# Latent attention with its queries prepared two heads ahead, and three kinds of small jobs handed to GpSimd

## The chip, the cores and the metric

The kernel runs on one core of a Trainium2 chip. The metric is device microseconds (us) of one execution, the median over several executions. One more execution was recorded by the hardware profiler; its trace gives the start and the length of nearly every instruction on each engine.

Five engines work side by side, each in the order of its own program: PE (TensorE) multiplies matrices and transposes, DVE (VectorE) and ACT (ScalarE) do the arithmetic on vectors, POOL (GpSimd) can do such arithmetic on data in SBUF too, and SP (SyncE) issues the transfers. They meet at semaphores: an instruction waits until a named counter has reached a value, and counts another one up when it is done.

## The reference: what is computed

The program is a four-layer transformer (256 latent tokens, 256 context tokens, width 1024), followed by a second block with 16 experts. The third layer's mixer is latent attention, and only that is touched:

```python
def mla_project(h, w_down, q_norm_g, kv_norm_g, w_uq, w_ukv, rope):
    cq, ckv, k_rope = jnp.split(h @ w_down, [MLA_Q_RANK, MLA_Q_RANK + MLA_KV_RANK], axis=-1)
    q = (rms_norm(cq, q_norm_g) @ w_uq).reshape(b, s, MLA_HEADS, MLA_NOPE_DIM + MLA_ROPE_DIM)
    kv = (rms_norm(ckv, kv_norm_g) @ w_ukv).reshape(b, s, MLA_HEADS, MLA_NOPE_DIM + MLA_V_DIM)
    ...
def mla_attend(q_nope, q_rope, k_nope, k_rope, v):
    scale = (MLA_NOPE_DIM + MLA_ROPE_DIM) ** -0.5
    s = (jnp.einsum("bqhd,bkhd->bhqk", q_nope, k_nope)
         + jnp.einsum("bqhr,bkr->bhqk", q_rope, k_rope)).astype(jnp.float32) * scale
    p = jax.nn.softmax(s, axis=-1)
    return jnp.einsum("bhqk,bkhe->bqhe", p.astype(v.dtype), v)
```

There are 16 heads. Each has 256 queries (two tiles of 128 rows) and 512 keys. The head outputs are then multiplied by `mla_w_o`.

## The kernel before: one turn per head, on four engines

**Exact products in three passes.** Each operand x is split into a high part (a rounded copy of type fp32r, made by ACT) and a low part (x minus the high part, made by DVE). A product is hi x hi + lo x hi + hi x lo: the three matmul lines L1847, L1848 and L1849. So every operand that is made on the way costs one ACT instruction and one DVE instruction. The weights are treated in the same way, in panels of 128x1024: `split_hi` (ACT, L1064) writes `w_hi`, `split_lo` (DVE, L2818) writes `w_lo` and counts up `panel_ready`. For that counter PE waits before it uses a panel, and SP before it loads new weights into the raw buffer.

**The turns.** `mla_attention` exists on ACT (L1532 on), PE (L2347 on) and DVE (L3451 on), and its order is written out by hand. Turn h belongs to head h:

- DVE takes the row maxima of both score tiles (`m_max`, L3493).
- ACT takes the exponentials (`mp_raw`, L1569), with the row sums beside them.
- DVE inverts the sums (`m_zinv`, L3502, counts up `z_inv`) and scales row tile 0 in place (L3504, `mla_norm0`). ACT scales row tile 1 in place (L1577, `mla_norm1`). PE waits for both before it transposes the weights (L2396).
- In the same turn the query of head h+1 is prepared: PE multiplies it out, DVE applies the rotary table (`mq_f`, L3461), ACT copies it (`mq_hi`, L1542), DVE subtracts (`mq_lo`, L3465). There is one buffer of each. Then PE can start the scores of head h+1.
- In turns 0 to 13 half of a pair of key tiles follows (`mk_hi` L1547, `mk_lo` L3471), then the output of head h-2 (`g_hi` L1583, `g_lo` L3514), then the two halves of the transposed weights of head h-1 (`mpt_hi` L1592, `mpt_lo` L3522).
- At the end of some turns stand value tiles (`h_hi` L1551, `h_lo` L3477; two in turns 0 and 1, one in turns 3 to 6) and weight panels (`splits`: turns 0, 1, 3, 6, 8, 14 and 15, one each).

PE's order in a turn: scores of head h, query of head h+1, keys (in even turns), weighted values of head h-2, transposes of head h-1, values. Scores and transposes each alternate between two PSUM banks, so that the scores of head h+1 may not be written before the exponentials of head h are taken. Query and value products share two banks. After turn 15 PE goes on with the weighted values of head 14 and, head pair by head pair, with the product with `mla_w_o` (`out_products`).

POOL has 8 subtractions in the first layer; in this layer 16 small copies and two subtractions before turn 0. After that it is idle to the end of the layer. DVE and POOL touch the same buffers nowhere in the turns.

## Time and profile before

| | us |
|---|---|
| median of 3 executions (2012.34 to 2015.85) | 2015.19 |
| the profiled execution, its own time | 2013.53 |
| its span, from the first to the last instruction | 2011.8 |
| PE busy | 1921.9 (96%) |
| DVE busy | 1531.0 (76%) |
| ACT busy | 1018.4 (51%) |
| POOL busy | 22.5 (1%) |
| from the first row maximum of turn 0 to that of turn 15, read at 1152.14 and 1250.07 | 97.93 |
| in these 97.93: DVE, PE and ACT busy | 82.57, 81.63, 71.96 |

All times in the text are microseconds from the start of the span. Busy times are sums over an engine's instructions; ends of matmuls are modelled, and consecutive instructions of one engine overlap a little in the record, so that the distance from start to start says more than the length. Over the whole program PE is busy for 96%; in the turns of this layer it is not, and the next section but one shows whom each engine waits for.

### The profile page before, as it was taken

How to read it: one execution, taken by the hardware profiler on the slowest of the kernel's cores; microseconds unless marked ns; L12 is line 12 of the kernel's file. 1: busy time of each engine (PE TensorE's matmuls, PEld its weight loads, DVE VectorE, ACT ScalarE, POOL GpSimd, SP SyncE). 2: the span in 40 equal slices, each digit the busy share in tenths (PEclk: the TensorE clock that was granted, in tenths of full speed). 3: DMA queues.
4: the chain of work that ended last, by engine and by line, in shares of the span. 5: the costliest groups of instructions: out<-in, count | busy, mean ns of one | idle time of the engine just before them, and what ended most of it. 6: DMA issues, size and time to landing. Idle time of an engine off the chain costs nothing.

```text
span 2011.8 us, 31051 instructions
## 1 busy us (share of the span) xinstructions
PE 1921.9 (96%) x11602; PEld 1684.5 (84%) x11602; DVE 1531.0 (76%) x2619; ACT 1018.4 (51%) x1721; POOL 22.5 (1%) x40
## 2 busy tenths in 40 slices
PE   6889999999999999999999777999999999999998
PEld 4687888889787888888888667999999999997886
DVE  3689888887667758777777588788887667876796
ACT  5353323245666656232333577655555546655685
POOL 0200000000000000000000100000000000000000
PEclk9999999999999999999999899999999999999999
DMA  7936455541211234557675220677645555426795
GB/s 291 321 119 232 165 209 188 188 168 48 84 64 63 67 112 139 169 186 244 236 244 158 58 73 27 227 268 261 207 135 189 168 169 168 134 67 236 260 354 195
DMA packets 265319, 346.67 MB, mean 172 GB/s; under 512 B 24167, under 2 KB 234962, under 8 KB 263778
## 3 DMA queue, kind: packets, MB, share of 16 engines
q1 hardware_dynamic: 265186, 344.90, 51.2%
q8 instruction: 84, 1.38, 0.3%
q14 instruction: 49, 0.40, 0.1%
HBM read 343.81 MB, written 1.06 MB: 171 GB/s over the span
## 4 chain that ended last, share of the span: by engine, by line
PE 75%; DVE 10%; ACT 6%; issue 5%; SPq 1%; DMA 1%; DVEq 0%; ACTq 0%
PE bank L1847 23%; PE bank L1848 23%; PE bank L1849 23%; PE bank L2663 2%; DVE w_lo L2818 2%; PE bank L2653 1%; ACT p_raw L1401 1%; ACT p_raw L1389 1%; DVE p_all L3297 1%; ACT norm L1157 1%; ACT w_hi L1064 1%; ACT mp_raw L1569 1%; DVE x L2886 1%; DVE neg_max L3306 1%; DVE norm L2844 1%
## 5 line engine op out<-in xcount | busy, mean ns | idle before, releaser
L2818 DVE TENSOR_TENSOR w_lo<-w_raw,w_hi 128x1024 fp32r<-128x1024 f32 x449 | 545.6, 1221 | 51.6 <-ACT w_hi L1064 24.9
L1064 ACT ACTIVATE w_hi<-w_raw 128x1024 fp32r<-128x1024 f32 x350 | 368.0, 1053 | 381.7 <-PE bank L1849 371.2
L1847 PE MATMUL bank<-h_hi,w_hi 128*128 128x512 f32 (+3 forms) x1360 | 466.9, 343 | 14.7 <-DVE w_lo L2818 8.6
L1848 PE MATMUL bank<-h_lo,w_hi 128*128 128x512 f32 (+3 forms) x1360 | 460.3, 338 | 0.0
L1849 PE MATMUL bank<-h_hi,w_lo 128*128 128x512 f32 (+3 forms) x1360 | 459.9, 338 | 0.0
L1847 PE MATMUL bank<-g_hi,w_hi 128*128 128x256 f32 (+1 forms) x1216 | 401.6, 330 | 7.2 <-DVE g_lo L3351 3.6
L1848 PE MATMUL bank<-g_lo,w_hi 128*128 128x256 f32 (+1 forms) x1216 | 399.6, 329 | 0.0
L1849 PE MATMUL bank<-g_hi,w_lo 128*128 128x256 f32 (+1 forms) x1216 | 399.5, 329 | 0.0
L1847 PEld LDWEIGHTS bank<-h_hi,w_hi 128*128 128x128 f32 x1360 | 257.9, 190 | 50.5 <-DVE w_lo L2818 10.8
L1849 PEld LDWEIGHTS bank<-h_hi,w_lo 128*128 128x128 f32 x1360 | 258.1, 190 | 27.7
L1848 PEld LDWEIGHTS bank<-h_lo,w_hi 128*128 128x128 f32 x1360 | 258.2, 190 | 26.4 <-issue 0.3
L1847 PEld LDWEIGHTS bank<-g_hi,w_hi 128*128 128x128 f32 x1216 | 231.8, 191 | 30.2 <-DVE g_lo L3351 4.5
L1849 PEld LDWEIGHTS bank<-g_hi,w_lo 128*128 128x128 f32 x1216 | 231.8, 191 | 20.3
L1848 PEld LDWEIGHTS bank<-g_lo,w_hi 128*128 128x128 f32 x1216 | 231.9, 191 | 19.7
L2971 DVE CUSTOM_DVE_ANT_0 mod_raw<-mod_raw,c_all,vec 128x1024 f32<-128x1024 f32 x160 | 203.0, 1278 | 0.0
L3016 DVE SCALAR_TENSOR_TENSOR x<-bank,mod,x 128x256 f32<-128x256 f32 x192 | 87.4, 479 | 85.1 <-PE bank L1849 79.8
L1304 ACT ACTIVATE norm<-bank 128x512 f32<-128x512 f32 x64 | 38.3, 598 | 189.4 <-PE bank L1849 189.4
L1744 ACT ACTIVATE w_hi<-w_raw 128x1024 fp32r<-128x1024 f32 x99 | 104.1, 1059 | 33.8 <-PE bank L1849 22.5
L3164 DVE TENSOR_TENSOR norm<-norm 128x512 f32<-128x512 f32 (+1 forms) x128 | 71.0, 555 | 54.2 <-ACT norm L1304 49.6
L2971 DVE CUSTOM_DVE_ANT_0 mod_prod<-mod_raw,c_all,vec 128x1024 f32<-128x1024 f32 x80 | 102.2, 1277 | 0.0
L3167 DVE TENSOR_TENSOR g_lo<-norm,g_hi 128x512 fp32r<-128x512 f32 (+1 forms) x128 | 71.5, 559 | 13.6 <-DVE norm L3164 0.5
L1847 PE MATMUL bank<-u_hi,w_hi 128*128 128x258 f32 x256 | 73.5, 287 | 0.0
(535 smaller groups left out, 2832.0 us busy)
## 6 DMA issues: line engine op xcount, KB each, us to landing
w_raw<-in_mlp_w SPq DMA_DIRECT2D x128, 1024.0 KB, 5.4
mod_raw<-in_mod_t SPq DMA_DIRECT2D x80, 1024.0 KB, 7.3
w_raw<-in_w_expert_gate SPq DMA_DIRECT2D x34, 512.0 KB, 4.7
w_raw<-in_w_expert_up SPq DMA_DIRECT2D x34, 512.0 KB, 5.8
w_raw<-in_w_expert_down SPq DMA_DIRECT2D x17, 1024.0 KB, 5.7
first_raw<-in_mod_w SPq DMA_DIRECT2D x16, 1024.0 KB, 5.9
w_raw<-in_diff_w_qkv SPq DMA_DIRECT2D x12, 1024.0 KB, 5.2
w_raw<-in_fourier_w SPq DMA_DIRECT2D x8, 1024.0 KB, 7.9
```

What stands on the lines that cost most here:

```text
L1064: act.activation(split_panel(W_hi[n % RING], n), raw_panel(n), ACT.Copy).then_inc(s("w_hi"), 1)
L1304: act.activation(relu[j % 2][:, 0:n_cols], bank[(t0 + j) % BANKS][:, 0:n_cols], ACT.Relu).then_inc(s("relu"), 1)
L1744: act.activation(W_hi[(p0 + n) % RING][:, :], raw_panel(p0 + n), ACT.Copy).then_inc(s("w_hi"), 1)
L1847: pe.matmul(dst, w_hi, r_hi, start=start, stop=False)
L1848: pe.matmul(dst, w_hi, r_lo, start=False, stop=False)
L1849: return pe.matmul(dst, w_lo, r_hi, start=False, stop=stop)
L2663: ins = pe.matmul(slot_out[half][:, :], e[x % 2][:, k, 0:P], v[:, w], start=x % 4 == 0 and k == 0 and q == 0, stop=x % 4 == 3 and k == 1 a ...
L2818: dve.tensor_tensor(split_panel(W_lo[n % RING], n), raw_panel(n), split_panel(W_hi[n % RING], n).bitcast(F32), ALU.subtract).then_inc(s("p ...
L2971: dve.tensor_tensor_reduce(mod_prod[:, :] if again else raw, raw, c_all[:, st, :], 1.0, bias, ALU.mult, ALU.add, mod[layer][:, t, st:st + ...
L3016: ins = dve.scalar_tensor_tensor(X[:, m, c], bank[t % BANKS][:, c], mod[layer][:, gate_at + m, st:st + 1], X[:, m, c], ALU.mult, ALU.add)
L3164: dve.tensor_tensor(squared, relu[j % 2][:, c], relu[j % 2][:, c], ALU.mult).then_inc(s("g_sq"), 1)
L3167: dve.tensor_tensor(G_lo[:, j, c], squared, G_hi[:, j, c].bitcast(F32), ALU.subtract).then_inc(s("g_lo"), 1)
```

## The change

Three things are done.

1. Queries two heads ahead. `mq_f`, `mq_hi` and `mq_lo` become two buffers each. Query 1 is made before turn 0, and turn h makes query h+2, on PE, DVE and ACT alike. On DVE the rotary product of head h waits for the subtraction of head h-2.
2. The second normalization (row tile 1, `mla_norm1`) moves from ACT to POOL: 16 instructions.
3. The low parts of the seven weight panels of this stage move from DVE to POOL, each behind the normalization of its turn. DVE waits for the last of them before the residual update behind the attention.

```diff
@@ mla_tiles
     add("q", 0, "mla_q", 1)
     add("k", 0, "mla_k_lo", 2)
-    for turn in range(MLA_HEADS - 1):
-        add("q", turn + 1, "mla_q", turn + 2)
+    add("q", 1, "mla_q", 2)
+    for turn in range(MLA_HEADS - 2):
+        add("q", turn + 2, "mla_q", turn + 3)
...
+MLA_SPLITS = {0: [2], 1: [3], 3: [4], 6: [5], 8: [6], 14: [7], 15: [8]}
...
@@ GpSimd
             swap_rotary(u + 2, 1)
+            p0 = PLAN.at["mla"]["panel"]
+            pool.wait_ge(s("panel_ready"), p0 + 2)
+            for turn in range(MLA_HEADS):
+                pool.wait_ge(s("z_inv"), BEFORE_MLA["z_inv"] + turn + 1)
+                pool.tensor_scalar(mp_raw[turn % 2][1][:, :], mp_raw[turn % 2][1][:, :], m_zinv[:, turn % 2, 1:2], None,
+                                   ALU.mult).then_inc(s("mla_norm1"), 1)
+                for n in MLA_SPLITS.get(turn, []):
+                    r = (p0 + n) % RING
+                    pool.wait_ge(s("w_hi"), p0 + n + 1)
+                    pool.tensor_tensor(split_panel(W_lo[r], p0 + n), raw_panel(p0 + n), split_panel(W_hi[r], p0 + n).bitcast(F32),
+                                       ALU.subtract).then_inc(s("panel_ready"), 1)
@@ ScalarE
                 query(0)
+                query(1)
                 for turn in range(MLA_HEADS + 2):
...
-                    if turn + 1 < MLA_HEADS:
-                        query(turn + 1)
+                    if turn + 2 < MLA_HEADS:
+                        query(turn + 2)
                     if turn // 2 + 1 < MLA_HEADS // 2:
                         keys(turn // 2 + 1, turn % 2)
-                    if on:
-                        act.wait_ge(s("z_inv"), BEFORE_MLA["z_inv"] + turn + 1)
-                        act.activation(mp_raw[turn % 2][1][:, :], mp_raw[turn % 2][1][:, :], ACT.Identity,
-                                       scale=m_zinv[:, turn % 2, 1:2]).then_inc(s("mla_norm1"), 1)
@@ TensorE
                 query_spread()
+                query(1)
                 for turn in range(MLA_HEADS):
                     scores(turn)
-                    if turn + 1 < MLA_HEADS:
-                        query(turn + 1)
+                    if turn + 2 < MLA_HEADS:
+                        query(turn + 2)
@@ VectorE
                 def query(h):
                     dve.wait_ge(s("tile_done"), t0 + MLA_TILE_AT["q", h] + 1)
-                    if h:
-                        dve.wait_ge(s("qk_lo"), BEFORE_MLA["qk_lo"] + h)
+                    if h >= 2:
+                        dve.wait_ge(s("qk_lo"), BEFORE_MLA["qk_lo"] + h - 1)
...
                 for j in range(2):
                     keys(0, j)
+                query(1)
+                query_lo(1)
...
-                    if turn + 1 < MLA_HEADS:
-                        query(turn + 1)
+                    if turn + 2 < MLA_HEADS:
+                        query(turn + 2)
...
-                    if turn + 1 < MLA_HEADS:
-                        query_lo(turn + 1)
+                    if turn + 2 < MLA_HEADS:
+                        query_lo(turn + 2)
...
-                    for n in splits.get(turn, []):
-                        split_lo_at(p0 + n)
...
             dve.memset(norm_buf[3][:, LAT:LAT + 2], 1.0).then_inc(s("down_inv"), 1)
+            dve.wait_ge(s("panel_ready"), PLAN.at["mla"]["panel"] + 9)
             output_added("mlao", 2, 1)
```

DVE in the first two turns, before. Each row is one instruction (x2: two in a row): line, operation, what is written from what. Numbers behind a name tell buffers apart:

```order
L3465 TENSOR_TENSOR mq_lo<-mq_f,mq_hi 128x256
L3471 TENSOR_TENSOR mk_lo_154<-bank,mk_hi_152 64x512
L3471 TENSOR_TENSOR mk_lo_155<-bank,mk_hi_153 64x512
L3493 TENSOR_REDUCE m_max<-bank 128x1 x2
L3461 TENSOR_TENSOR mq_f<-bank,q_table 128x256
L3502 RECIPROCAL m_zinv<-m_z 128x2
L3504 TENSOR_SCALAR mp_raw_140<-mp_raw_140,m_zinv 128x512
L3465 TENSOR_TENSOR mq_lo<-mq_f,mq_hi 128x256
L3471 TENSOR_TENSOR mk_lo_154<-bank,mk_hi_152 64x512
L3477 TENSOR_TENSOR h_lo<-bank,h_hi 128x512 x2
L2818 TENSOR_TENSOR w_lo_63<-w_raw_68,w_hi_59 128x1024
L3493 TENSOR_REDUCE m_max<-bank 128x1 x2
```

The same place on DVE in the changed kernel (its line numbers are a little higher):

```order
L3485 TENSOR_TENSOR mk_lo_158<-bank,mk_hi_156 64x512
L3474 TENSOR_TENSOR mq_f_150<-bank,q_table 128x256
L3478 TENSOR_TENSOR mq_lo_154<-mq_f_150,mq_hi_152 128x256
L3508 TENSOR_REDUCE m_max<-bank 128x1 x2
L3474 TENSOR_TENSOR mq_f_149<-bank,q_table 128x256
L3517 RECIPROCAL m_zinv<-m_z 128x2
L3519 TENSOR_SCALAR mp_raw_140<-mp_raw_140,m_zinv 128x512
L3478 TENSOR_TENSOR mq_lo_153<-mq_f_149,mq_hi_151 128x256
L3485 TENSOR_TENSOR mk_lo_157<-bank,mk_hi_155 64x512
L3491 TENSOR_TENSOR h_lo<-bank,h_hi 128x512 x2
L3508 TENSOR_REDUCE m_max<-bank 128x1 x2
```

A second query stands ahead of the first maxima, `mq_lo` keeps its place directly behind the scaling of row tile 0, and the panel subtraction is gone from the end of the turn.

POOL in the changed kernel, from its last small copies to the end of turn 3. Before, nothing stands between these copies and the next layers' work:

```order
L1027 COPY w_raw_66<-w_raw_66 128x4x2x8 x8
L1048 TENSOR_SCALAR mp_raw_141<-mp_raw_141,m_zinv 128x512
L1053 TENSOR_TENSOR w_lo_63<-w_raw_68,w_hi_59 128x1024
L1048 TENSOR_SCALAR mp_raw_143<-mp_raw_143,m_zinv 128x512
L1053 TENSOR_TENSOR w_lo_64<-w_raw_65,w_hi_60 128x1024
L1048 TENSOR_SCALAR mp_raw_141<-mp_raw_141,m_zinv 128x512
L1048 TENSOR_SCALAR mp_raw_143<-mp_raw_143,m_zinv 128x512
L1053 TENSOR_TENSOR w_lo_61<-w_raw_66,w_hi_57 128x1024
```

So POOL scales once per turn, when `z_inv` is counted up, which is what DVE's own scaling of row tile 0 waits for as well; a panel subtraction delays the scaling of the next turn if it takes too long.

## Rows read from the trace of the kernel before

**Rows 1.** Waits, 1140 to 1285: engine and line waited for whom; us, times, longest
```profile
ACT mp_raw L1569 <- DVE m_max L3493: 27.6, 17, 2.3
PEld bank L1847 <- DVE mq_lo L3465: 21.1, 15, 3.2
DVE m_zinv L3502 <- ACT mp_raw L1569: 9.4, 16, 0.9
DVE m_max L3493 <- PE bank L1849: 1.7, 2, 1.1
```

**Rows 2.** DVE's timeline, turns 10 to 12: start, us, instruction, [idle before it <- releaser]
```profile
1220.30 1.28 DVE L3493 TENSOR_REDUCE m_max<-bank 128x1 f32<-128x512 f32 x2
...
1225.85 1.28 DVE L3493 TENSOR_REDUCE m_max<-bank 128x1 f32<-128x512 f32 x2
...
1228.05 0.17 DVE L3502 RECIPROCAL m_zinv<-m_z 128x2 f32<-128x2 f32 x1 [0.59 <-ACT mp_raw L1569]
1228.25 0.49 DVE L3504 TENSOR_SCALAR mp_raw<-mp_raw,m_zinv 128x512 f32<-128x512 f32 x1
1228.65 0.42 DVE L3465 TENSOR_TENSOR mq_lo<-mq_f,mq_hi 128x256 fp32r<-128x256 f32 x1
1229.10 0.69 DVE L3471 TENSOR_TENSOR mk_lo<-bank,mk_hi 64x512 fp32r<-64x512 f32 x1
1230.12 0.43 DVE L3514 TENSOR_TENSOR g_lo<-bank,g_hi 64x256 fp32r<-64x256 f32 x1 [0.33 <-ACT g_hi L1583]
1230.74 1.29 DVE L3522 TENSOR_TENSOR mpt_lo<-bank,mpt_hi 128x512 fp32r<-128x512 f32 x2 [0.19 <-ACT mpt_hi L1592]
1231.95 1.28 DVE L3493 TENSOR_REDUCE m_max<-bank 128x1 f32<-128x512 f32 x2
```

**Rows 3.** ACT's timeline in turn 11
```profile
1228.96 0.72 ACT L1577 ACTIVATE mp_raw<-mp_raw,m_zinv 128x512 f32<-128x512 f32 x1
```

**Rows 4.** DVE's timeline, the panel subtraction that ends turn 8
```profile
1213.05 1.22 DVE L2818 TENSOR_TENSOR w_lo<-w_raw,w_hi 128x1024 fp32r<-128x1024 f32 x1
1214.20 1.28 DVE L3493 TENSOR_REDUCE m_max<-bank 128x1 f32<-128x512 f32 x2
```

**Rows 5.** DVE's timeline, the first maxima of turn 0 and those of turn 15
```profile
1152.14 0.69 DVE L3493 TENSOR_REDUCE m_max<-bank 128x1 f32<-128x512 f32 x1 [1.07 <-PE bank L1849]
...
1250.07 1.28 DVE L3493 TENSOR_REDUCE m_max<-bank 128x1 f32<-128x512 f32 x2
```

**Rows 6.** POOL's timeline, where DVE works on SBUF at the same time
```profile
58.81 2.79 POOL L1027 TENSOR_TENSOR h_lo<-norm,h_hi 128x512 fp32r<-128x512 f32 x2 [3.09 <-ACT h_hi L1254]
...
1137.60 1.30 POOL L1035 TENSOR_TENSOR mk_lo<-kr_f,mk_hi 64x512 fp32r<-64x512 f32 x1
```

**Rows 7.** DVE's timeline at the same times
```profile
59.97 1.92 DVE L3051 SCALAR_TENSOR_TENSOR g_lo<-four_raw,scale_mix,g_hi 128x254 fp32r<-128x254 f32 x2 [1.10 <-ACT g_hi L1237]
...
1137.96 1.50 DVE L3432 TENSOR_TENSOR ckv_lo<-ckv_f,ckv_hi 128x512 fp32r<-128x512 f32 x1 [0.70 <-ACT ckv_hi L1518]
```

**Rows 8.** Single lines: count, shortest/median/longest ns, first and last start
```profile
L3051 DVE SCALAR_TENSOR_TENSOR g_lo<-four_raw,scale_mix,g_hi x16: 468/480/1518, 43.2 to 62.2; 128x254 fp32r<-128x254 f32 x16
L1022 POOL COPY w_raw<-w_raw x16: 231/233/1235, 1107.0 to 1142.6; 128x64 f32<-128x64 f32 x16
```

**Rows 9.** POOL's groups by line: busy us, mean ns | idle before
```profile
L1043 POOL TENSOR_SCALAR_AFFINE_SELECT qs<-qs 64x512 f32<-64x512 f32 x2 | 1.3, 657 | 597.0 <-ACT qs L1692 597.0
L1005 POOL MEMSET silu_c<- 128x256 f32 x1 | 0.3, 313 | 0.0
L1002 POOL MEMSET ones<- 128x128 f32 x1 | 0.2, 206 | 0.0
```

**Rows 10.** Timelines of ACT and PE behind the maxima of turn 15
```profile
1254.59 1.06 ACT L1064 ACTIVATE w_hi<-w_raw 128x1024 fp32r<-128x1024 f32 x1
...
1255.08 0.36 PE L1847 MATMUL bank<-mpt_hi,h_hi 128*128 128x256 f32 x1 [4.21 <-DVE mpt_lo L3522]
...
1258.40 0.41 PE L1847 MATMUL bank<-g_hi,w_hi 128*128 128x256 f32 x1
```

More of the change, by code:

```diff
@@ L559, in build_program @@
         ckv_hi, ckv_lo = sb("ckv_hi", [P, TOK], F32R), sb("ckv_lo", [P, TOK], F32R)
-        mq_f = sb("mq_f", [P, LAT])
-        mq_hi, mq_lo = sb("mq_hi", [P, LAT], F32R), sb("mq_lo", [P, LAT], F32R)
+        mq_f = [sb(f"mq_f{j}", [P, LAT]) for j in range(2)]
+        mq_hi = [sb(f"mq_hi{j}", [P, LAT], F32R) for j in range(2)]
+        mq_lo = [sb(f"mq_lo{j}", [P, LAT], F32R) for j in range(2)]
         mk_hi = [sb(f"mk_hi{j}", [P, TOK], F32R) for j in range(2)]
@@ L1541, in query @@
                     act.wait_ge(s("mla_q"), h + 1)
-                    act.activation(mq_hi[:, :], mq_f[:, :], ACT.Copy).then_inc(s("qk_hi"), 1)
+                    act.activation(mq_hi[h % 2][:, :], mq_f[h % 2][:, :], ACT.Copy).then_inc(s("qk_hi"), 1)
                 def keys(pair, j):
@@ L1595, in mla_attention @@
                         values(i)
-                    for n in splits.get(turn, []):
+                    for n in MLA_SPLITS.get(turn, []):
                         if n == 4:
@@ L2385, in scores @@
                         q = slice(i * P, (i + 1) * P)
-                        split_product(dst[:, :], mq_hi[:, q], mq_lo[:, q], mk_hi[h % 2][:, :], mk_lo[h % 2][:, :],
+                        split_product(dst[:, :], mq_hi[h % 2][:, q], mq_lo[h % 2][:, q], mk_hi[h % 2][:, :], mk_lo[h % 2][:, :],
                                       True, True).then_inc(s("aux_done"), 1)
@@ L3458, in query @@
                     dve.wait_ge(s("tile_done"), t0 + MLA_TILE_AT["q", h] + 1)
-                    if h:
-                        dve.wait_ge(s("qk_lo"), BEFORE_MLA["qk_lo"] + h)
-                    dve.tensor_tensor(mq_f[:, :], made("q", h)[:, 0:LAT], q_table[:, h % 2, :], ALU.mult).then_inc(s("mla_q"), 1)
+                    if h >= 2:
+                        dve.wait_ge(s("qk_lo"), BEFORE_MLA["qk_lo"] + h - 1)
+                    dve.tensor_tensor(mq_f[h % 2][:, :], made("q", h)[:, 0:LAT], q_table[:, h % 2, :], ALU.mult).then_inc(s("mla_q"), 1)
                 def query_lo(h):
                     dve.wait_ge(s("qk_hi"), BEFORE_MLA["qk_hi"] + h + 1)
-                    dve.tensor_tensor(mq_lo[:, :], mq_f[:, :], mq_hi[:, :].bitcast(F32), ALU.subtract).then_inc(s("qk_lo"), 1)
+                    dve.tensor_tensor(mq_lo[h % 2][:, :], mq_f[h % 2][:, :], mq_hi[h % 2][:, :].bitcast(F32),
+                                      ALU.subtract).then_inc(s("qk_lo"), 1)
                 def keys(pair, j):
@@ L3478, in values @@
                                       ALU.subtract).then_inc(s("v_lo"), 1)
-                splits = {0: [2], 1: [3], 3: [4], 6: [5], 8: [6], 14: [7], 15: [8]}
                 query(0)
@@ L3524, in mla_attention @@
                         values(i)
-                    for n in splits.get(turn, []):
-                        split_lo_at(p0 + n)
             norm_rest("mix2", TOK)
```

1 line of the change is left out of this document (removed).

## The prediction, made before the changed kernel ran

> **What bounds the kernel now.** Read the busy shares first: PE 96% over the program, so that most edits off PE are worth nothing. Then read them for the stage that is changed. From the first maxima of turn 0 to those of turn 15 [rows 5] lie 97.93 us, of which PE is busy for 81.63 and DVE for 82.57: nobody is full there, so a loop over several engines sets the pace. The waits of this stretch show which [rows 1]. PE waits for `mq_lo` for 21.1 us, which looks like the bound, but DVE waits for PE's scores only twice, 1.7 us in all: PE is early whatever the query costs. ACT waits 27.6 us for `m_max`, and DVE 9.4 us in 16 waits for the exponentials. So the loop is DVE to ACT and back to DVE, with everything else that DVE must do in a turn.
>
> DVE's timeline shows the turn [rows 2]. Turn 10 takes 1225.85 - 1220.30 = 5.55, turn 11 takes 1231.95 - 1225.85 = 6.10. Counted from the maxima: inversion of the sums at 2.20, after 0.59 of idling for the exponentials; scaling of row tile 0 at 2.40; `mq_lo` at 2.80; `mk_lo` at 3.25; `g_lo` at 4.27 after 0.33 of waiting for ACT; `mpt_lo` after 0.19 more. In turn 10 these last two waits are missing. They exist because ACT has its own normalization, 0.72 us long, ahead of `g_hi` and `mpt_hi` [rows 3].
>
> **The change, part by part.**
>
> *Normalization off ACT.* ACT reaches `g_hi` about 0.6 to 0.7 earlier. The waits of 0.33 and 0.19 go, and a turn like 11 becomes one like 10: 0.55 each. What is late next is DVE itself.
>
> *Panel subtractions off DVE.* From its start to the next maxima one takes 1214.20 - 1213.05 = 1.15 [rows 4]. Six of the seven end turns ahead of turn 15 (0, 1, 3, 6, 8, 14), 6.9 us, with some tenths of waiting for `w_hi` in front; ACT's part stays, and lies in its idle time before the next exponentials.
>
> *Queries two ahead.* PE may begin scores earlier, but DVE hardly waits for them, so by itself this is worth nothing on DVE's path. It has a use as cover: with ACT faster, transposes would be late next, as they follow the scores on PE; now the scores need not wait for `mq_lo`. Ahead of turn 0 DVE gets one query more, some 0.7 us, in the 1.07 that it idles there [rows 5]; nothing. Turn 14 loses its query.
>
> I rebuild the 15 turns instead of adding differences: 15 x 5.55 = 83.25. Eight value tiles at 0.60 (half of the 1231.95 - 1230.74 = 1.21 for the two equal subtractions of rows 2) add 4.8. Turn 0 has no `g_lo` and no `mpt_lo`, but waits for PE's second scores: -1.1. Turn 1 has no `g_lo`: -0.5. Turn 14 has neither query nor keys: -1.1. Sum 85.35, against 97.93: a gain of 12.6, if POOL's work were free.
>
> *What POOL costs DVE.* It is not free, and this is the term that I rest most on. POOL subtracted from 1137.60 to 1138.90 [rows 6]; DVE's `ckv_lo`, both inputs in SBUF, began at 1137.96 and took 1.50 [rows 7], where two equal subtractions with one input in PSUM take 1.29 together. It ended 0.56 behind POOL's end, so it stood still to 0.13 before that end. In the first layer POOL's pair of subtractions ran from 58.81 to 61.60, and two of DVE's L3051 from 59.97 to 61.89; the second of them took 1.518 instead of the median 0.480 [rows 6 to 8], so that it began at 60.37. And POOL's copies, 0.231 each, took up to 1.235 [rows 8]. So one of the two stands still while the other works on SBUF. The second case shows more: POOL's first subtraction was over at about 60.1, DVE's first instruction ran, and then POOL's second subtraction got in ahead of DVE's second instruction. The Trainium skill ("SBUF — State Buffer", "Who interferes with whom") states this as a rule: a VectorE instruction with two SBUF inputs, or one in a two-port mode, and a GpSimd instruction that reads SBUF exclude each other for the whole instruction. By that rule, with which the trace agrees, work moved to GpSimd is not free where VectorE is the bound.
>
> In each turn POOL's normalization is released by the same `z_inv` as DVE's scaling, and behind that stands `mq_lo`, with both inputs in SBUF. The scaling does 512 columns in 0.49, where a subtraction of 512 takes 0.65 to 0.69, so it runs in a faster mode and I take it to exclude POOL too. Then: scaling 2.40 to 2.89; POOL's normalization gets in; `mq_lo` stands still. Should POOL come first, the scaling stands still instead, with the same sum. How long? The trace of before has no such operation on POOL. Nearest rows [rows 9]: 512 elements with one input, the selection on 64 rows, 0.657; memsets of 128 and 256 elements 0.206 and 0.313, so 0.84 ns an element and 0.10 fixed, 0.53 for 512. As its start-up lies beside the scaling, I let it end 0.5 behind the scaling, at 3.39, and `mq_lo` start again 0.15 before that: 3.24 instead of 2.80, x = 0.45. The lower end is x = 0 (no exclusion, or `mq_lo` slips in first); the upper end the two-input subtraction's 1.30 in full: 2.89 + 1.30 - 0.15 - 2.80 = 1.24. I take 0.45, since it has one input. Turns 0 to 13 have a `mq_lo`: 14 x 0.45 = 6.3.
>
> The Trainium skill ("GPSIMD Engine Reference", "Performance versus the Vector engine") gives two-input work 2.6 cycles an element and a simple one-input body between 1.03 and 1.8 cycles at 1.2 GHz. An estimate from that page: 0.44 to 0.77 us for the normalization, x of about 0.4 to 0.7, and a gain between 3.6 and 7.8 us.
>
> *Panels on POOL.* Twice 1.30, 2.6 us, for 1024 elements. In turn 8 ACT's high part would be ready near 5.3, POOL done near 7.9, and DVE's next scaling comes at 5.55 + 0.45 + 2.40 = 8.4. No overlap, and DVE's instructions in between have one input in PSUM or are maxima. If x were 0, it would touch the scaling by some tenths in a few turns. Bounds: 0 to 0.5 in each of six turns; I take 0. SP's reloads wait for `panel_ready` 1.4 us longer; nothing is short there.
>
> *The tail.* PE starts the weighted values of head 14 at 1255.08, 5.01 behind the maxima of turn 15, after 4.21 of idling [rows 10]. ACT's normalization (0.72) and with it DVE's waits behind it fall away, and POOL's gets no `mq_lo` to hold up here: I expect 4.0. But the last panel is now cut by POOL: `w_hi` begins 4.52 behind the maxima [rows 10], after the change about 3.6, ends 4.7, POOL ends 7.3. PE wanted it at 1258.40, 8.33 behind them, and would want it near 7.3. So 0.8 of the 1.0 is kept; ends 0 and 1.0.
>
> *Sum.* 12.6 - 6.3 + 0.8 = 7.1 faster. 2013.53, the profiled execution's own time, becomes 2006.4. The median of the runs, 2015.19, is 1.66 above that execution, so 2008.1; I say 2008.
>
> **The rivals.**
>
> *Nothing stands still (B).* The scaling does not exclude POOL, or `mq_lo` goes first: x near 0.1 at most. For: DVE issues `mq_lo` before the scaling has ended (2.80 against 2.89). Against: in rows 6 and 7 POOL got in between. Gain 13.4 less about 1 for x and touches of panels: 12.4, time 2002.8.
>
> *POOL is slow at this operation (C).* A scaling by a column read from SBUF may cost more than a selection. x from 0.67 to 1.2: 13.4 - 14 x 0.95 = 0.1. Time 2015.
>
> *POOL at its two-input rate, with nothing of it beside DVE's scaling (D), the slower side.* Place: `mq_lo` behind the scaling, 14 times. Price: x = 1.24, 17.4 against the 13.4 gained, 4.0 slower, time 2019.2. The break-even is x = 13.4 / 14 = 0.96, a normalization that ends 1.1 behind DVE's scaling. For: every POOL arithmetic row of 512 elements with two inputs has 1.28 to 1.30. Against: this one has one input, and both one-input rows are at half of that.
>
> *PE takes over (E).* The weighted values of head h-1 need the last `mpt_lo` of turn h, then come the transposes that ACT needs near 3.3 of the next turn. By my count PE is done 1.4 before that. PE's 81.63 of busy time are under my 85.35 + 6.3, but its order is strict; 0.25 a turn would give back 3.7. Time 2011.8. That the queries ahead do nothing is no rival: in my sum they are worth nothing alone.
>
> **How the numbers follow.** Forecast (A) 0.45, B 0.13, C 0.18, D 0.12, E 0.12. About 0.2%, 4.0 us, is what a measurement can tell from no change. Faster than that: A nearly whole, B, half of E: 0.62. Within: a little of A, C, a third of D, half of E: 0.30. Slower: the rest of D, 0.08. The range leaves out the far part of B below and D above: 2001.5 to 2016. A by itself, x from 0.25 to 0.67: 2005 to 2011.
>
> **What would show it.** In the profile after: DVE's `mq_lo` (128x256, 0.42 now) near 0.9, or its scaling longer than 0.49, in turns 0 to 13, ending just behind POOL's normalization; without it, B. POOL's normalization 0.5 to 0.9 long including its own standing still. No `w_lo` on DVE between the turns, no wait of `g_lo` and `mpt_lo` for ACT. Even turns of about 6.0 instead of 5.55, odd ones of 6.0 instead of 6.10, and 91 to 92 us between the first maxima of turn 0 and those of turn 15. `m_max` waiting for PE in most turns would mean E. A stage that is shorter with an unchanged total would mean that a later stage gives it back; I see none, as PE is the bound behind it.

## The result, and the profile after

The changed kernel took 1999.07 us (median of 4 runs, 1996.75 to 1999.88). Beside it on the same chip the kernel before took 2013.76. The ratio is 0.992, with a 95% interval of 0.9907 to 0.9933: 14.7 us faster, where 7.1 had been forecast, and below the low end of the range. The profiled execution took 1999.88, its span is 1998.2, against 2013.53 and 2011.8 before. Of the three parts of the change two hand work to POOL (the second normalization and the low parts of the panels), where the title counts three; the third, the queries two heads ahead, stays on its engines.

The 97.93 us between the first maxima of turn 0 and those of turn 15 [rows 5] became 1236.26 - 1153.39 = 82.87. DVE's timeline of the changed kernel (columns as in [rows 2]) shows both ends:

```profile
1153.39 1.28 DVE L3508 TENSOR_REDUCE m_max<-bank 128x1 f32<-128x512 f32 x2
...
1236.26 1.27 DVE L3508 TENSOR_REDUCE m_max<-bank 128x1 f32<-128x512 f32 x2
```

The waits between 1153 and 1236.5 answer to [rows 1] (engine and line waited for whom; us in total, times, longest):

```profile
ACT mp_raw L1585 <- DVE m_max L3508: 20.7, 14, 1.9
DVE m_zinv L3517 <- ACT mp_raw L1585: 9.3, 15, 0.9
PEld bank L1859 <- DVE g_lo L3529: 5.9, 6, 2.0
PE bank L1859 <- DVE mpt_lo L3537: 4.9, 9, 1.6
```

The loop of DVE and ACT is still there, DVE never waits for scores, and PE no longer waits for `mq_lo`. Turns 10 and 11 on DVE answer to [rows 2]:

```profile
1210.38 1.28 DVE L3508 TENSOR_REDUCE m_max<-bank 128x1 f32<-128x512 f32 x2
...
1213.18 0.42 DVE L3478 TENSOR_TENSOR mq_lo<-mq_f,mq_hi 128x256 fp32r<-128x256 f32 x1
1213.52 0.68 DVE L3485 TENSOR_TENSOR mk_lo<-bank,mk_hi 64x512 fp32r<-64x512 f32 x1
1214.12 0.41 DVE L3529 TENSOR_TENSOR g_lo<-bank,g_hi 64x256 fp32r<-64x256 f32 x1
1214.45 1.27 DVE L3537 TENSOR_TENSOR mpt_lo<-bank,mpt_hi 128x512 fp32r<-128x512 f32 x2
1215.64 1.27 DVE L3508 TENSOR_REDUCE m_max<-bank 128x1 f32<-128x512 f32 x2
1216.84 0.41 DVE L3474 TENSOR_TENSOR mq_f<-bank,q_table 128x256 f32<-128x256 f32 x1
1217.83 0.17 DVE L3517 RECIPROCAL m_zinv<-m_z 128x2 f32<-128x2 f32 x1 [0.58 <-ACT mp_raw L1585]
1218.03 0.49 DVE L3519 TENSOR_SCALAR mp_raw<-mp_raw,m_zinv 128x512 f32<-128x512 f32 x1
1218.43 0.42 DVE L3478 TENSOR_TENSOR mq_lo<-mq_f,mq_hi 128x256 fp32r<-128x256 f32 x1
1218.88 0.69 DVE L3485 TENSOR_TENSOR mk_lo<-bank,mk_hi 64x512 fp32r<-64x512 f32 x1
1219.50 0.42 DVE L3529 TENSOR_TENSOR g_lo<-bank,g_hi 64x256 fp32r<-64x256 f32 x1
1219.95 1.29 DVE L3537 TENSOR_TENSOR mpt_lo<-bank,mpt_hi 128x512 fp32r<-128x512 f32 x2
1221.16 1.28 DVE L3508 TENSOR_REDUCE m_max<-bank 128x1 f32<-128x512 f32 x2
```

The two waits for ACT in turn 11 are gone, as foreseen. But `mq_lo` takes its old 0.42, not 0.9, and the turns last 5.26 and 5.52, not 6.0. POOL's timeline shows who stood still instead, in turn 11 and in turns 14 and 15, which have no `mq_lo`:

```profile
1218.09 2.11 POOL L1048 TENSOR_SCALAR mp_raw<-mp_raw,m_zinv 128x512 f32<-128x512 f32 x1 [3.14 <-DVE m_zinv L3517]
...
1234.39 1.86 POOL L1048 TENSOR_SCALAR mp_raw<-mp_raw,m_zinv 128x512 f32<-128x512 f32 x1 [3.41 <-DVE m_zinv L3517]
1236.35 2.38 POOL L1053 TENSOR_TENSOR w_lo<-w_raw,w_hi 128x1024 fp32r<-128x1024 f32 x1
1238.71 1.85 POOL L1048 TENSOR_SCALAR mp_raw<-mp_raw,m_zinv 128x512 f32<-128x512 f32 x1
```

POOL's scaling is 0.25 longer in the turns that have a `mq_lo`. It is also slow in itself, 1.86 where I had estimated 0.53 to 0.66, but it has 5.3 us for it.

By stages, read from the same two traces (stage: from the first product with `q_table` to the first residual `x` behind the attention; us):

| | before | after | gain |
|---|---|---|---|
| ahead of the maxima of turn 0 | 4.51 | 4.73 | -0.22 |
| maxima of turn 0 to those of turn 15 | 97.93 | 82.87 | 15.06 |
| from there to the first residual | 20.81 | 19.38 | 1.43 |
| the stage | 123.25 | 106.98 | 16.27 |

The executions differ by 13.65. The missing 2.6 us lie outside the stage, in work that the change leaves alone (1.03 ahead of it, 1.6 behind it); single executions of a kernel spread by as much.

Part of the 16.27 goes with TensorE's granted clock and not with the change. The clock has two levels, 1.2 and 2.4 GHz, and its mean over a stretch is given here as a share of the full one. The changed kernel's profiled execution had 1.00 in all 15 turns and behind them. The one of before had 0.91 in turn 0, 0.94 in turn 8 and 0.92 behind the turns, and in its turn 0 DVE waited for PE's second scores, which the changed kernel's doesn't do:

```profile
1153.42 0.69 DVE L3493 TENSOR_REDUCE m_max<-bank 128x1 f32<-128x512 f32 x1 [0.59 <-PE bank L1849]
```

An estimate: 0.6 for that wait, and 0.7 behind the turns, which is what lies between the two last kernels of the next section (19.37 at a clock of 1.00, 20.05 at 0.91, with the same program from turn 1 on). That makes about 1.3 of the 16.27. Whether the change has a part in when the clock rises isn't shown.

### The profile page after: what moved, and what is told of

The parts are those of the page before. It is cut to its first block, busy times and chain, and to the rows that moved or that the text cites. A ratio compares the mean times of both kernels' runs of the same rounds, so it can differ in the third digit from the quotient of the medians.

```text
span 1998.2 us, 31052 instructions
## 1 busy us (share of the span) xinstructions
PE 1919.7 (96%) x11602; PEld 1684.6 (84%) x11602; DVE 1521.1 (76%) x2612; ACT 1006.6 (50%) x1705; POOL 72.3 (4%) x63
## 4 chain that ended last, share of the span: by engine, by line
PE 75%; DVE 11%; ACT 5%; issue 5%; DMA 1%; SPq 1%; POOL 0%; DVEq 0%; ACTq 0%
PE bank L1859 23%; PE bank L1861 22%; PE bank L1860 22%; PE bank L2676 2%; DVE w_lo L2831 2%; PE bank L2666 1%; ACT p_raw L1417 1%; ACT p_raw L1405 1%; DVE p_all L3310 1%; ACT norm L1173 1%; ACT mp_raw L1585 1%; DVE mpt_lo L3537 1%; DVE x L2899 1%; DVE neg_max L3319 1%; DVE norm L2857 1%
## 5 line engine op out<-in xcount | busy, mean ns | idle before, releaser
L2831 DVE TENSOR_TENSOR w_lo<-w_raw,w_hi 128x1024 fp32r<-128x1024 f32 x442 | 537.5, 1222 | 50.4 <-ACT w_hi L1080 24.4
L1859 PE MATMUL bank<-h_hi,w_hi 128*128 128x512 f32 (+3 forms) x1360 | 467.1, 343 | 14.7 <-DVE w_lo L2831 8.6
```

The source lines that it names most:

```text
L1859: pe.matmul(dst, w_hi, r_hi, start=start, stop=False)
L2831: dve.tensor_tensor(split_panel(W_lo[n % RING], n), raw_panel(n), split_panel(W_hi[n % RING], n).bitcast(F32), ALU.subtract).then_inc(s("p ...
```

## The experiments

Each was compared with runs of the kernel before on the same chip (medians 2013.76 to 2015.16). "Turns" is the time between the two maxima above, 97.93 before and 82.87 after; "stage" is that of the table; "clock" is the mean granted clock in the turns (0.98 before). Medians of different rows come from different sets of runs, whose medians of before differ by up to 1.4 us, so that a difference of a few us between two rows has to be seen in the ratios too: the intervals of lo_on_pool and keys_early overlap that of the changed kernel. Turns and stage are from one execution each, and a stretch of low clock in it can make one turn about 1 us longer (turn 2 of norm_on_act at 0.74: 6.50, where the other even turns without a value tile take 5.55).

| kernel | median | ratio to before (95%) | turns | stage | clock |
|---|---|---|---|---|---|
| changed kernel | 1999.07 | 0.9920 (0.9907, 0.9933) | 82.87 | 106.98 | 1.00 |
| lo_late | 2002.68 | 0.9938 (0.9925, 0.9952) | 88.73 | 112.84 | 0.95 |
| gap_before_lo | 2004.12 | 0.9957 (0.9941, 0.9973) | 90.22 | 114.35 | 0.97 |
| norm_on_act | 2007.14 | 0.9959 (0.9946, 0.9973) | 90.92 | 115.97 | 0.97 |
| panels_on_dve | 2004.96 | 0.9950 (0.9937, 0.9964) | 89.82 | 114.55 | 0.98 |
| query_one_ahead | 1999.26 | 0.9915 (0.9901, 0.9928) | 84.33 | 108.21 | 0.98 |
| only_norm | 2005.87 | 0.9956 (0.9943, 0.9970) | 93.00 | 116.02 | 0.96 |
| only_panels | 2007.75 | 0.9963 (0.9949, 0.9976) | 90.72 | 117.34 | 0.98 |
| only_queries | 2015.03 | 1.0001 (0.9992, 1.0010) | 97.78 | 124.24 | 0.97 |
| lo_on_pool | 1996.30 | 0.9912 (0.9896, 0.9927) | 81.27 | 105.35 | 0.98 |
| keys_early | 1996.24 | 0.9900 (0.9883, 0.9917) | 80.37 | 104.46 | 0.97 |
| both_moves | 1993.19 | 0.9893 (0.9877, 0.9908) | 78.81 | 102.90 | 0.98 |
| both_but_first | 1991.07 | 0.9884 (0.9869, 0.9899) | 76.06 | 100.83 | 0.99 |

### Why does `mq_lo` not stand still?

**lo_late.** The changed kernel with `mq_lo` behind `mk_lo`, so that it starts 1.1 to 1.4 us behind POOL's scaling instead of 0.35.

```diff
-                    if turn + 2 < MLA_HEADS:
-                        query_lo(turn + 2)
                     if turn // 2 + 1 < MLA_HEADS // 2:
                         keys(turn // 2 + 1, turn % 2)
+                    if turn + 2 < MLA_HEADS:
+                        query_lo(turn + 2)
```

> The changed kernel with one edit: in DVE's turn `mq_lo` stands behind `mk_lo` instead of ahead of it, so it begins near 3.2 instead of 2.65 behind the maxima, when POOL's scaling has been running for some 0.8 us. Theory 1 (POOL takes its first data only some tenths after its start, DVE's two instructions slip in before, and whoever is late stands still): `mq_lo` stands still until about 0.15 before POOL's scaling ends, some 1.2 us long instead of 0.42, POOL's scaling is down from 2.11 to 1.86; turns of 6.1 instead of 5.4, 14 times, so 10 to 11 us slower than the changed kernel, near 2010. Theory 2 (POOL's scaling by a column gives way to DVE whenever DVE comes): `mq_lo` stays at 0.42, POOL's scaling stays at 2.11, no change in time (within 2 us of 1999).

DVE's timeline, an even turn and the middle of the odd one behind it, and POOL's scaling in the even one:

```profile
1193.35 0.49 DVE L3519 TENSOR_SCALAR mp_raw<-mp_raw,m_zinv 128x512 f32<-128x512 f32 x1
1193.93 0.68 DVE L3485 TENSOR_TENSOR mk_lo<-bank,mk_hi 64x512 fp32r<-64x512 f32 x1
1194.54 0.41 DVE L3478 TENSOR_TENSOR mq_lo<-mq_f,mq_hi 128x256 fp32r<-128x256 f32 x1
...
1200.11 0.69 DVE L3485 TENSOR_TENSOR mk_lo<-bank,mk_hi 64x512 fp32r<-64x512 f32 x1 [0.24 <-ACT mk_hi L1563]
```

```profile
1193.41 1.86 POOL L1048 TENSOR_SCALAR mp_raw<-mp_raw,m_zinv 128x512 f32<-128x512 f32 x1 [4.71 <-DVE m_zinv L3517]
```

Nobody stands still: `mq_lo` takes 0.41 though POOL's record runs on to 1195.27, and POOL is back at 1.86. Neither theory had that. What POOL reads must be read by 1194.54, 0.73 ahead of the end of its record. The kernel is slower than the changed one for other reasons: `mk_lo` now comes before ACT has its high part (0.24 in an odd turn), and its turn 2, at a clock of 0.74, is 1.24 longer than the changed kernel's. So this run doesn't say what happens to `mq_lo` while POOL does read; the next one does.

Its first two turns show two things besides, POOL first, then DVE:

```profile
1155.95 1.77 POOL L1048 TENSOR_SCALAR mp_raw<-mp_raw,m_zinv 128x512 f32<-128x512 f32 x1 [11.60 <-DVE m_zinv L3517]
1158.93 2.39 POOL L1053 TENSOR_TENSOR w_lo<-w_raw,w_hi 128x1024 fp32r<-128x1024 f32 x1 [1.21 <-ACT w_hi L1080]
1161.30 1.73 POOL L1048 TENSOR_SCALAR mp_raw<-mp_raw,m_zinv 128x512 f32<-128x512 f32 x1
```

```profile
1155.80 0.49 DVE L3519 TENSOR_SCALAR mp_raw<-mp_raw,m_zinv 128x512 f32<-128x512 f32 x1
1160.99 0.62 DVE L3519 TENSOR_SCALAR mp_raw<-mp_raw,m_zinv 128x512 f32<-128x512 f32 x1
```

First, POOL's scaling begins 0.15 and 0.31 behind DVE's in these two turns, and 0.06 in most others, and takes 1.77, 1.73 and 1.86; but in all 16 turns it ends 1.43 behind the end of DVE's scaling. So POOL waits until DVE's scaling is through, and is ready for its data no later than 0.31 after its own start. Second, in turn 1 POOL's subtraction of a panel runs into DVE's scaling, and the scaling takes 0.62 instead of 0.49: as if it had begun at 1161.12, 0.20 before the end of the panel's record. Here it is DVE that stands still.

**gap_before_lo.** The changed kernel with one small maximum between DVE's scaling and `mq_lo`; its result goes to a spare buffer that nothing reads.

```diff
+                        dve.tensor_reduce(gap_out[:, 0:1], q_table[:, 0, 0:P], AX.X, ALU.max)
                         query_lo(turn + 2)
```

> The changed kernel with one small DVE instruction more in turns 0 to 13 (a maximum over 128 columns of `q_table`, written to a spare column) between DVE's scaling of row tile 0 and `mq_lo`. It touches neither POOL's data nor, by the rows of before, what POOL is kept out by. It moves `mq_lo` to some 0.6 us behind the start of POOL's scaling; in the changed kernel it stands at 0.35 behind it (POOL's scaling is 0.25 longer for it, DVE not at all), in `lo_late` at 1.1 behind it (neither is longer). Theory 3 (first come, first served: POOL waits out DVE's scaling, and gets its data as soon as DVE leaves a gap; `mq_lo` went ahead in the changed kernel only because it followed the scaling without a gap): `mq_lo` is 0.6 to 0.9 long instead of 0.42, POOL's scaling 1.86 instead of 2.11; turns longer by 0.2 for the small instruction and 0.2 to 0.5 for the stall, 6 to 10 us in all over the changed kernel. Theory 4 (POOL's scaling gives way to DVE in every case): `mq_lo` 0.42, POOL's scaling near 2.11, only the small instruction's 0.2 a turn, 3 us.

DVE's timeline of one turn, POOL's of the same turn, and all `mq_lo` (count, shortest/median/longest ns, first and last start):

```profile
1216.83 0.49 DVE L3520 TENSOR_SCALAR mp_raw<-mp_raw,m_zinv 128x512 f32<-128x512 f32 x1
1217.23 0.28 DVE L3523 TENSOR_REDUCE gap_out<-q_table 128x1 f32<-128x128 f32 x1
1217.42 0.72 DVE L3479 TENSOR_TENSOR mq_lo<-mq_f,mq_hi 128x256 fp32r<-128x256 f32 x1
```

```profile
1216.88 1.86 POOL L1049 TENSOR_SCALAR mp_raw<-mp_raw,m_zinv 128x512 f32<-128x512 f32 x1 [4.16 <-DVE m_zinv L3518]
```

```profile
L3479 DVE TENSOR_TENSOR mq_lo<-mq_f,mq_hi x16: 424/718/720, 1149.2 to 1234.9; 128x256 fp32r<-128x256 f32 x16
```

Now `mq_lo` takes 0.72 and POOL its 1.86: the stall has changed sides. The turns are 0.50 longer than the changed kernel's (5.76 and 6.00 against 5.26 and 5.51), which is 0.20 for the added instruction and 0.30 for the stall. So the two engines do exclude each other. Without a gap `mq_lo` stands directly behind the scaling, which POOL is waiting for too, and it goes ahead of POOL; a gap of 0.2 us is enough for POOL to get in. From the length, `mq_lo` really began near 1217.42 + 0.30 = 1217.72, 0.84 behind the start of POOL's record and 1.02 ahead of its end: up to there POOL's scaling keeps it out, and it agrees with lo_late. That the added maximum lengthens `mq_lo` by itself wasn't tested apart; `mq_f`, which follows the maxima of every turn, takes its 0.41 there.

"Who comes first goes first" is not what these runs show. In turn 11 of the changed kernel POOL's scaling begins at 1218.09 and was ready at 1218.40 at the latest; `mq_lo` begins at 1218.43 and still goes ahead. Nor does DVE always keep its turn when its next instruction is at hand. The pair of the first layer, whose instructions [rows 6] and [rows 7] show together, reads singly, in the kernel before:

```profile
59.97 0.48 DVE L3051 SCALAR_TENSOR_TENSOR g_lo<-four_raw,scale_mix,g_hi 128x254 fp32r<-128x254 f32 x1 [1.10 <-ACT g_hi L1237]
60.06 1.55 POOL L1027 TENSOR_TENSOR h_lo<-norm,h_hi 128x512 fp32r<-128x512 f32 x1
60.37 1.52 DVE L3051 SCALAR_TENSOR_TENSOR g_lo<-four_raw,scale_mix,g_hi 128x254 fp32r<-128x254 f32 x1
```

DVE's second instruction begins 0.40 behind its first and 0.08 before the first has ended, exactly as `mq_lo` does behind the scaling, and POOL begins 0.09 behind the first. Here POOL gets in, and DVE's second stands still for 1.04. The instructions differ on both engines (DVE: two inputs of 254 columns instead of one input of 512; POOL: two inputs instead of one and a column), and no run changed one of these alone. What decides who goes first stays open.

### What is each part worth?

Three kernels undo one part of the change, three more have one part alone.

**norm_on_act.** The second normalization back on ACT.

```diff
-                pool.tensor_scalar(mp_raw[turn % 2][1][:, :], mp_raw[turn % 2][1][:, :], m_zinv[:, turn % 2, 1:2], None,
-                                   ALU.mult).then_inc(s("mla_norm1"), 1)
@@ ScalarE
+                        act.activation(mp_raw[turn % 2][1][:, :], mp_raw[turn % 2][1][:, :], ACT.Identity,
+                                       scale=m_zinv[:, turn % 2, 1:2]).then_inc(s("mla_norm1"), 1)
```

> The changed kernel with the second normalization back on ACT (queries ahead and panels on POOL kept). If ACT's 0.72 us ahead of `g_hi` and `mpt_hi` is what made turns 5.55 and 6.10 long: turns go from 5.26 and 5.52 back to about 5.5 and 6.1, 15 turns, 5 to 7 us slower, 2004 to 2006. If the queries ahead had removed that wait already (rival): no change.

8.1 us slower than the changed kernel by the medians, somewhat more than expected; in the profiled executions 8.05 in the turns and 0.95 behind them. Some 1.0 of the 8.05 is turn 2 at the low clock; behind the turns both executions had 1.00. DVE's timeline, the end of an odd turn with the even turn behind it:

```profile
1202.52 0.43 DVE L3530 TENSOR_TENSOR g_lo<-bank,g_hi 64x256 fp32r<-64x256 f32 x1 [0.33 <-ACT g_hi L1596]
1203.14 1.29 DVE L3538 TENSOR_TENSOR mpt_lo<-bank,mpt_hi 128x512 fp32r<-128x512 f32 x2 [0.20 <-ACT mpt_hi L1605]
1204.35 1.28 DVE L3509 TENSOR_REDUCE m_max<-bank 128x1 f32<-128x512 f32 x2
...
1207.48 0.68 DVE L3486 TENSOR_TENSOR mk_lo<-bank,mk_hi 64x512 fp32r<-64x512 f32 x1
1208.20 0.42 DVE L3530 TENSOR_TENSOR g_lo<-bank,g_hi 64x256 fp32r<-64x256 f32 x1
1208.69 1.29 DVE L3538 TENSOR_TENSOR mpt_lo<-bank,mpt_hi 128x512 fp32r<-128x512 f32 x2
1209.89 0.68 DVE L3509 TENSOR_REDUCE m_max<-bank 128x1 f32<-128x512 f32 x1
```

The odd turn has the waits of [rows 2] again. The even turn lists no wait, and is nevertheless 5.54 long against 5.26 with the normalization on POOL. Compare the starts with turn 10 of the changed kernel: `mk_lo` to `g_lo` 0.72 against 0.60, `g_lo` to `mpt_lo` 0.49 against 0.33, together the 0.28. So a turn that seemed to be DVE's alone was still held by ACT, by amounts too small to be listed.

**panels_on_dve.** The low parts of the panels back at the ends of DVE's turns.

```diff
-                for n in MLA_SPLITS.get(turn, []):
-                    r = (p0 + n) % RING
-                    pool.wait_ge(s("w_hi"), p0 + n + 1)
-                    pool.tensor_tensor(split_panel(W_lo[r], p0 + n), ...
...
@@ VectorE
                         values(i)
+                    for n in MLA_SPLITS.get(turn, []):
+                        split_lo_at(p0 + n)
```

> The changed kernel with the seven panel subtractions back on DVE (queries ahead and normalization on POOL kept). If DVE alone sets the turn: six subtractions of 1.15 come back between the maxima, plus some tenths of waiting for `w_hi`: 7 to 8 us slower than the changed kernel, 2006 to 2007. If they were hidden by another wait in the changed kernel, under 4 us.

5.9 us slower in the medians; 6.95 in the turns, where 6 panels at the forecast's 1.15 are 6.9, and 0.63 behind them, where this execution had a clock of 0.91 and the changed kernel's 1.00: that part says nothing about the panel. A turn with a panel is 1.13 or 1.14 longer than its counterpart (turn 0 6.28 against 5.15, turn 8 6.39 against 5.26).

**query_one_ahead.** The kernel before with the normalization and the panels moved, and its one query buffer kept. Against the changed kernel, on PE, DVE and ACT alike (the buffers and the second query ahead of turn 0 are left out here):

```diff
-                    if turn + 2 < MLA_HEADS:
-                        query(turn + 2)
+                    if turn + 1 < MLA_HEADS:
+                        query(turn + 1)
```

> The changed kernel with queries only one head ahead again (normalization and panels on POOL kept). By the prediction's sum the queries ahead are worth nothing alone, but cover the transposes: without them PE begins the scores of head h+1 behind `mq_lo`, at 3.0 of the turn, and ends the transposes near 8.2 to 8.9, 2.9 to 3.6 into the next turn, where ACT wants them at 2.9. I expect waits of `mpt_hi` for the transposes, 0.2 to 0.6 in about half of the turns, so 2 to 5 us slower, 2001 to 2004. Rival: the second buffer set is what the gain rests on, over 8 us slower. Rival: no use at all, within 1 us.

1999.26, the changed kernel's time. The stage is 1.23 longer, at the two ends of the turns (turn 0 by 0.90, turn 1 by 0.21, turn 14 by 0.34, less 0.22 ahead of them); from turn 2 to turn 13 every turn is within 0.01 of the changed kernel's. PE waits for `mq_lo` again, and DVE waits for scores no more than before, 1.7 us in 2 waits. In turn 0, where 0.90 of the 1.23 lies, the clock was 0.77 against 1.00, and gap_before_lo, with its queries two ahead and a clock of 0.89 there, has a wait for the second scores too. So not even this 0.90 is shown to come from the queries. At full clock they weren't needed as cover either. Of a stretch of low clock there is one pair: turn 8 with panels on DVE takes 7.46 with one query ahead (only_norm, clock 0.82, ACT waits 0.9 for PE) and 6.39 with two (panels_on_dve, clock 1.00). But turn 2 of lo_late, with two ahead and a clock of 0.74, is about 1 us too long as well, so the clock is the nearer cause.

**only_norm, only_panels, only_queries.** The kernel before with one part of the change each, their edits those of the diff ahead of the prediction.

> The kernel before with only the second normalization on POOL (queries one head ahead, panels on DVE). If the parts add up as undoing them one by one says (8.1 us of the timed median for this one), 2006 to 2007.5, turns of 5.26 and 5.51 where no panel or value tile stands. Rival (with one query buffer the transposes come late, the cover that the prediction gave the queries): turns over 5.5 and under 5 us gained, 2010.

> The kernel before with only the seven panel subtractions on POOL. 6 subtractions of 1.15 and the waits ahead of them go from between the maxima: 7 to 8 us faster than before, near 2007; turns stay at 5.55 and 6.10 where no value tile stands, since ACT's normalization stays. Rival (undoing it alone gave 5.9 of the median, so part of it is covered by something): 5 to 6 us.

> The kernel before with only the queries two heads ahead. The prediction's sum gave this nothing; undoing it alone left the later turns at 5.26 and 5.51 and cost 1.2 us of the stage, all in the first turns, with nothing to be seen in the median. So within 1.5 us of before, PE's wait for `mq_lo` (21.1 us) gone and replaced by other waits. Rival: over 3 us faster.

By the medians, against the same runs of the kernel before: 9.2 faster, 7.3 faster, and 0.0 (ratio 1.0001, interval 0.9992 to 1.0010, 11 runs). Together 16.5, against the 14.7 of all three: they add up to within the spread of the runs. In the turns of the profiled executions they don't: 4.93, 7.21 and 0.15 make 12.3, and all three together give 15.06. The missing 2.8 lie in turns 0 and 8, where only_norm takes 8.14 and 7.46 at clocks of 0.75 and 0.82, and the changed kernel 5.15 and 5.26 at 1.00. The waits of only_queries, 1140 to 1285, tell why they are worth nothing alone:

```profile
PEld bank L1852 <- DVE g_lo L3522: 19.1, 13, 4.3
PE bank L1852 <- DVE mpt_lo L3530: 14.7, 12, 4.1
```

PE's 21.1 us of waiting for `mq_lo` [rows 1] are gone; PE has moved on to the next thing that DVE owes it.

### Where does the rest go?

If DVE sets the turns, less on DVE must pay. DVE still waits 9.3 us for the exponentials, 0.58 a turn, and that idle time could be filled.

**lo_on_pool.** `mq_lo` on POOL, behind its scaling.

```diff
...
+                if turn + 2 < MLA_HEADS:
+                    h = turn + 2
+                    pool.wait_ge(s("qk_hi"), BEFORE_MLA["qk_hi"] + h + 1)
+                    pool.tensor_tensor(mq_lo[h % 2][:, :], mq_f[h % 2][:, :], mq_hi[h % 2][:, :].bitcast(F32),
+                                       ALU.subtract).then_inc(s("qk_lo"), 1)
@@ VectorE
-                    if turn + 2 < MLA_HEADS:
-                        query_lo(turn + 2)
```

> The changed kernel with `mq_lo` of heads 2 to 15 moved from DVE to POOL, behind POOL's scaling of the same turn; with queries two ahead there is a whole turn for it. If DVE alone sets the turn, each of 14 turns loses the 0.33 to 0.45 from `mq_lo` to `mk_lo`: 5 to 6 us faster than the changed kernel, near 1994. Rival (PE takes over near 5.0 a turn, or POOL's three jobs, 1.9 + 0.8 + 2.4, overrun the turn where a panel stands): under 3 us.

2.8 us faster than the changed kernel by the medians, about half of what I expected, and with overlapping intervals of the ratios; 1.6 in the turns. Steady turns are 5.11 and 5.38, 0.13 to 0.15 shorter where 0.34 to 0.45 was taken off. DVE now comes to `mk_lo` before ACT's `mk_hi` (1.4 us of listed waits in 6 turns, and small ones besides).

**keys_early.** The key tile goes ahead of the exponentials on ACT and into DVE's idle time ahead of the inversion.

```diff
@@ ScalarE
+                    if turn // 2 + 1 < MLA_HEADS // 2:
+                        act.wait_ge(s("aux_done"), attention_tile("mla", "score", turn, 1)[0])
+                        keys(turn // 2 + 1, turn % 2)
@@ VectorE
                         query(turn + 2)
+                    if turn // 2 + 1 < MLA_HEADS // 2:
+                        keys(turn // 2 + 1, turn % 2)
...
```

> The changed kernel with the key halves made earlier in the turn: ACT copies `mk_hi` ahead of the exponentials (it idles there for 0.9 to 1.7), and DVE subtracts `mk_lo` between `mq_f` and the inversion of the sums, where it idles for 0.59. If DVE alone sets the turn, 0.6 goes in 14 turns, 8 us, near 1991. Rival (PE is next: its products of a turn need 4.6 to 5.3, 5.0 on average, against 5.39): 5.39 - 5.0 = 0.4 a turn at most, 5 to 6 us faster, near 1994, with DVE waiting for PE's scores in most turns. Rival (ACT's copy delays the first exponential): nothing.

2.8 us faster than the changed kernel by the medians, less than either side expected, with single runs from 1990.56 to 1997.07. Steady turns fall to 4.67 and 5.07. But turn 0 takes 8.19, since the keys of turn 0 now stand in front of its exponentials and PE has not made them yet: ACT waits 9.6 us for key products in 9 waits.

**both_moves** joins the two, **both_but_first** keeps the keys of turn 0 at their old place.

```diff
+                    if turn and turn // 2 + 1 < MLA_HEADS // 2:
...
+                    if turn == 0:
+                        keys(1, 0)
```

> Both edits together: `mq_lo` on POOL and the keys early. DVE alone would need 4.3 to 4.5 a turn, so this shows the next bound. If that is PE: no more than `keys_early` gives, near 1993 to 1994. If DVE were still the bound: 13 us under the changed kernel, near 1986.

> `both_moves`, but in turn 0 the key half stays where the changed kernel has it, since there PE has not made the key tile yet (turn 0 took 7.99 instead of 5.15 in `both_moves`). If that is all: turn 0 near 5.2 and some 2.5 us faster than `both_moves`, near 1990.5. Rival (PE is full in turns 0 to 4, so that what turn 0 gains the next turns give back): within 1 us of it.

1993.19 and 1991.07; in the turns 2.75 lie between the two, as expected. The last is 8.0 us faster than the changed kernel, with intervals that lie apart, and beats both single moves. Turn 0 is back at 5.57, steady turns are 4.62 to 4.89. Its waits, 1150 to 1232:

```profile
ACT mk_hi L1570 <- PE bank L1871: 8.3, 10, 1.6
ACT mp_raw L1595 <- DVE m_max L3518: 4.9, 6, 1.5
DVE m_zinv L3529 <- ACT mp_raw L1595: 4.1, 8, 0.9
```

ACT's wait for DVE has fallen from 20.7 to 4.9 and a wait for PE stands first: DVE no longer sets the pace alone. That PE's key products are the next bound is argued from these waits; no run made them cheaper.

## Why the prediction was wrong, step by step

**The loop of DVE and ACT, and PE's 21.1 us: right.** Removing PE's wait alone gives 0.0 (only_queries).

**Panels, 1.15 each: right.** 6.9 forecast for the turns, 6.95 measured by undoing it. One panel on POOL takes 2.38, 2.6 was forecast, and DVE's 16 scalings all stay between 485 and 489 ns, so that no panel touched one, as forecast. It was close: in lo_late a panel holds the scaling of turn 1 up.

**The step that failed: "POOL's normalization gets in; `mq_lo` stands still", x = 0.45, 14 times, 6.3 us.** In the changed kernel x is 0: `mq_lo` takes its 0.42 in all of turns 0 to 13, and the 6.3 us are simply gained. The exclusion is there: with a gap ahead of `mq_lo` it stands still for 0.30 (gap_before_lo). What the prediction had wrong is the order. I had seen POOL get in between two DVE instructions in the first layer [rows 6 to 8] and took it for the rule. I mentioned what spoke against it, that `mq_lo` is issued before the scaling has ended (2.80 against 2.89), and gave it a chance of 0.13 without working it out. It could not have been worked out from those rows: in the first layer DVE's second instruction was issued just as early, and POOL got in all the same. Behind the scaling `mq_lo` goes first, and why stays open. What POOL then costs is paid by POOL, 0.25 a turn, and POOL has time. So rival B was the true one, in its second form; its time of 2002.8 was still 3.7 too long.

The size of x, had POOL got in, was near by luck. gap_before_lo lets `mq_lo` begin 0.89 behind the start of the scaling, where it begins 0.40 behind in the changed kernel: an estimate of 0.5 for x. Two errors cancelled in my 0.45: POOL's scaling is 1.86 long and not 0.53 to 0.66 (the 0.53 came from memsets, which read nothing), and it lets DVE in 1.02 before the end of its record and not 0.15. For POOL's subtractions the 0.15 was about right, 0.20 in lo_late. Rivals C and D (0.30 of the chance together) took that length as the price; it is longer than D's 1.30, and costs DVE nothing.

**The base turn of 5.55: too long, 2.5 us.** 85.35 was rebuilt for the turns, 82.87 measured. By turns: the six even ones from 2 to 12 were 0.29 shorter than forecast, 1.74 together; turn 0 was 5.15 where 5.55 + 1.2 - 1.1 = 5.65 was forecast, 0.5, since the wait for PE's second scores that I had kept in it didn't come, at the full clock; the rest 0.24. I had taken turn 10 as free of ACT because no wait stood in it. norm_on_act shows that it was not. The odd turns, whose waits are listed, came out as forecast: 5.51 against 5.55. Why they are 0.25 longer than the even ones is only argued, below.

**The tail: 1.43 instead of 0.8.** PE's timeline has both points:

```profile
1240.46 0.35 PE L1859 MATMUL bank<-mpt_hi,h_hi 128*128 128x256 f32 x1 [2.04 <-DVE mpt_lo L3537]
...
1243.40 0.39 PE L1859 MATMUL bank<-g_hi,w_hi 128*128 128x256 f32 x1 [0.55 <-POOL w_lo L1053]
```

The values of head 14 begin 4.20 behind the maxima of turn 15 (4.0 forecast, 5.01 before), the last panel's product 7.14 behind them (7.3 forecast, 8.33 before [rows 10]). The wait of 0.55 for POOL's last panel is the predicted collision. The excess of 0.6 need not come from the change: before, the clock was 0.92 behind the turns, after 1.00, and with such a stretch of low clock both_but_first takes 0.7 more there than both_moves.

**Queries two ahead: worth nothing alone, right; their use as cover, not borne out.** Without them the transposes are not late either (query_one_ahead). The 1.2 us at the two ends of the turns are within the spread of whole runs, and 0.9 of them lie in a turn with a lower clock.

The sum closes: forecast for the turns 12.6 - 6.3 = 6.3; 6.3 for x and 2.5 for the base turn come back, 15.1 in all; with 1.4 for the tail and -0.2 ahead of the turns 16.3 in the stage, about 1.3 of it with the clock. Of the 16.3, 13.65 shows between the two profiled executions and 14.7 between the medians.

## What to carry to other kernels

When two engines exclude each other, price both orders, and ask which engine has the slack to stand still: the same exclusion cost nothing with two DVE instructions back to back and 0.30 us a turn with 0.2 us between them, and back to back was no safeguard in the first layer. Before adding up stages of single executions, compare the granted clock turn by turn. Don't calibrate a loop's shortest turn on one without listed waits; compare the distances from start to start with those of the same pair elsewhere. An engine's long wait is worth nothing as long as nobody waits for that engine: 21 us of it could be removed for 0.0.
